# Differential attention by token tile, woven into its two projections, with three changes at the stage boundaries

## The chip, the cores and the metric

The kernel runs on one core of a Trainium2 chip. The metric is the device time of one execution in microseconds (us), the median of several runs. The five engines of the core are named as the profile names them: PE (TensorE, matmuls), DVE (VectorE), ACT (ScalarE), POOL (GpSimd) and SP (SyncE, which here only issues transfers).

## The reference

256 tokens of width 1024 pass through two transformer layers and a hybrid block. The change is in the second layer's differential attention and in how each stage hands over to the next. The attention computes, for 8 heads of two score maps each (64 wide) and values 128 wide:

```python
q = (x @ w_q).reshape(B, S, 2 * H, DH).transpose(0, 2, 1, 3) * (DH ** -0.5)
lam = jnp.exp(jnp.sum(lv[0] * lv[1])) - jnp.exp(jnp.sum(lv[2] * lv[3])) + lam_init
...
s = jnp.einsum('bhqd,bhkd->bhqk', qi, k_sh).astype(jnp.float32)
s = jnp.where(key_pos[None, :] <= qpos[:, None], s, -jnp.inf)
a = jax.nn.softmax(s, axis=-1).reshape(B, H, 2, Q_BLOCK, S)
diff = a[:, :, 0] - lam * a[:, :, 1]
return jnp.einsum('bhqk,bhkv->bhqv', diff.astype(v_sh.dtype), v_sh)
...
o = rms_norm(o, subln) * (1.0 - lam_init)
return o @ w_out
```

## The kernel before

The tokens form two tiles of 128 (tile 0 and tile 1). The network is a row of stages, in this order: F0, MI, MO, F1, P0, KV, F2, DQ, the attention, DO, F3, P1, HI, HC, HA, HO. F0 to F3 are feed-forward blocks, DQ and DO the query and the output projection of the differential attention, P0 and P1 gated projections, KV the shared keys and values, HI to HO the hybrid block. Each float32 matmul of a projection is done as three: a rounded high part and a remainder of both operands (`w_hi`, `w_lo`, `xT_hi`, `xT_lo`) are multiplied as hi by hi, lo by hi and hi by lo.

Weights come in slots of 512 KB (128 partitions by 2048). SP issues the transfers into `w_raw` (3 buffers), ACT casts a slot to `w_hi` (L536), POOL subtracts to get `w_lo` in four parts (L507), and there are 6 split slots. ACT's casts stand at fixed places of its program: `ahead(slot)` casts the slot four ahead. A projection of 1024 by 1024, DQ or DO, is 4 slots; each slot is 12 matmuls of 512 columns for one tile (`across_tile`, L1593 to L1595: four k, three matmuls each). Each engine's program is written out by hand, and each engine runs it strictly in order; semaphores tie them.

A stage boundary works so: ACT takes the sums of squares of a tile's output (`post_sum`), DVE makes the norm and adds into the residual (`boundary`, L1055 and L1056), PE transposes the residual (`t_of_x`, L1640), DVE scales the transposes by the gain, ACT rounds them to `xT_hi` (`t_hi`), DVE subtracts to get `xT_lo` (L1021). `pre_sum` and `pre_norm` make the following stage's norm. The transposes land in the PSUM banks that `t_bank` names. PSUM has eight banks: `acc` (4), `gu` (2), `tb` (2).

In the attention, one step handles one head for both tiles: PE computes four score blocks into `tb` (a = 0, partitions 0 to 63 of the operands) and `gu` (a = 1, partitions 64 to 127) (L1923), DVE adds the mask and takes the maxima, writing the scores to SBUF (L1308), ACT does four exps (L783), DVE forms the difference of the two softmaxes (L1315 to L1325), PE transposes it (L1931), ACT copies it (L791), PE multiplies by the values (L1940 to L1942), ACT copies the result (L797) and sums its squares (L802). The steps are pipelined over three to four heads; between DQ's last matmul and DO's first one nothing else stands on PE.

Of the kernel before, what the change touches and what calls it, by code (L numbers as in the profile page):

```python
# [26 lines left out]
I32 = mybir.dt.int32  # L27
# [15 lines left out]
AHEAD = 4  # L43
PART = 512
# [68 lines left out]

def psum_units(u):

    return u + 1 - (4 if u >= 4 * T["HC"] else 0)


def program(nc, A, out):
    ctx = ExitStack()  # L120
    with ctx:
# [60 lines left out]
        sc_ = area(6144, 2, 768)  # L182
        dif = area(7680, 2, LCOLS)
        difT = area(8448, 2, LCOLS)
# [50 lines left out]
        bg_bc = sb("bg_bc", [P, 8])  # L235

# [103 lines left out]
        d_lamexp = sem("d_lamexp")  # L340
        d_qn_ready = sem("d_qn_ready")
# [37 lines left out]
        def _(sp):  # L379
# [57 lines left out]
            def linear(s0, w, cols, halves_first=False):  # L437
# [3 lines left out]
                if halves_first:  # L441
                    order = [(c, j) for j in range(2) for c in cols]
# [22 lines left out]
            linear(S["DO"], A["diff_w_out"][0], both, halves_first=True)  # L465
# [35 lines left out]


# [20 lines left out]
        def _(act):  # L523
# [23 lines left out]
            def sum_of(j, t, src):  # L547
                if 2 * j + t:
                    act.wait_ge(sums_ready, 2 * j + t)
                nc.scalar.activation(squares[:], src, ACT.Square,  # L550
                                     accum_out=ssq[:, 2 * j + t:2 * j + t + 1]).then_inc(sums_ready, 1)
# [17 lines left out]
            def boundary(following, post_sum, between=lambda: None, late=lambda: None):  # L569
# [192 lines left out]
            def diff():  # L762
                s0 = S["DQ"]
                ahead(At(s0 + 1))
# [3 lines left out]
                for w in range(4):  # L768
                    if w == 2:
                        ahead(At(s0 + 3))  # L770
                    act.wait_ge(d_pl_in_psum, w + 1)
                    nc.scalar.copy(qT[:, 4 * (w % 2):4 * (w % 2) + 4, tok(w // 2)],
                                   tb[:, w % 2, :].rearrange("p (k c) -> p k c", k=4)).then_inc(d_pl_ready, 1)
                for step in range(DH + 3):
                    h = step
                    if h < DH:
                        act.wait_ge(d_negmax, 4 * h + 4)
                        for t in range(TILES):
                            for a in range(2):

                                e = sc_[:, h % 2, LCOLS * a + P * t:LCOLS * a + P * t + P * (t + 1)]
                                i = 2 * t + a
                                ins = nc.scalar.activation(e, e, ACT.Exp, scale=-1.0, bias=dstat[:, h % 2, 4 + i:5 + i],  # L783
                                                           accum_out=dstat[:, h % 2, 8 + i:9 + i])
                        ins.then_inc(d_exped, 1)
                    h = step - 2
                    if 0 <= h < DH:
                        act.wait_ge(d_dt_in_psum, h + 1)
                        if h >= 2:
                            act.wait_ge(d_o_in_psum, h - 1)  # L790
                        nc.scalar.copy(difT[:, h % 2, :], acc[:, 0, 512 * (h % 2):512 * (h % 2) + LCOLS]  # L791
                                       ).then_inc(d_dt_ready, 1)
                    h = step - 3
                    if 0 <= h < DH:
                        act.wait_ge(d_o_in_psum, h + 1)
                        src = acc[:, 1, 512 * (h % 2):512 * (h % 2) + 2 * P].rearrange("p (t c) -> p t c", t=2)
                        nc.scalar.copy(qn[:, :, tok(h)], src)  # L797
                        if h:
                            act.wait_ge(d_o_ready, h)
                        for t in range(TILES):  # L800
                            i = 8 * (h // 4) + 4 * t + h % 4
                            ins = nc.scalar.activation(squares[:, tok(t)], src[:, t, :], ACT.Square,  # L802
                                                       accum_out=hstat[:, i:i + 1])
                        ins.then_inc(d_o_ready, 1)
                act.wait_ge(d_o_ready, DH)
                t_hi("DO", 0)
                t_hi("DO", 1)
                out_linear("DO", "F3")
# [132 lines left out]
            for w in range(4):  # L941
# [4 lines left out]
                if w == 1:  # L946
# [5 lines left out]
            ahead(At(S["F2"]))  # L952
            ffn("F2", "DQ")
            act.wait_ge(x_ready, x_count(4, 1, 1))
            load_gain(A["norm_g"][1, 3])
            act.dma_start(lamv, A["diff_lambda"][0].rearrange("(o a) d -> o (a d)", o=1).broadcast_to([P, 256])
                          ).then_inc(d_landed, 16)
            act.dma_start(subln, A["diff_subln"].rearrange("o d -> d o")).then_inc(d_landed, 16)
# [11 lines left out]
        def _(dve):  # L970
# [24 lines left out]
            def norm_steps(j, t):  # L995
                i = 2 * j + t
                dve.wait_ge(sums_ready, i + 1)
# [1122 lines left out]
```

## Time and profile before

| | |
|---|---|
| median of 3 runs | 1438.81 us (1438.66 to 1441.03) |
| the profiled execution's own time | 1435.71 us |
| its span | 1433.8 us |
| PE busy | 1379.3 us (96%) |
| POOL busy | 1135.1 us (79%) |
| ACT busy | 659.8 us (46%) |
| DVE busy | 461.1 us (32%) |
| mean granted TensorE clock | 0.988 |

Busy times are sums over the whole span. The differential attention with its two projections is a small part of it, so its own stretches have to be read for what it costs. Brackets in a timeline row give the idle time of the engine ahead of that row and what ended it; a duration there is from the start of the record to its end, and where matmuls follow each other the distance of two starts is what one costs.

### The profile page before, as it was taken

The page shows a single profiled execution, that of the slowest core. Times are in us where ns is not written, and L with a number is a line of the kernel's source. Part 1 is how long each engine was busy: PE and PEld are TensorE (multiplying, and loading weights), DVE is VectorE, ACT ScalarE, POOL GpSimd, SP SyncE. Part 2 cuts the span into 40 slices and gives each one's busy share as a digit, 9 for nine tenths or more (in the row PEclk, how much of TensorE's full clock was granted, in tenths as well). Part 3 has the DMA queues.
Part 4 walks back from the last instruction along what each step waited for, and adds up shares of the span by engine and source line. Part 5 has one row for each costly group of instructions (what it writes and reads, how often), then busy time and mean ns, then how long its engine had stood idle before and what let it go on. Part 6 is the DMA issues. An engine that isn't in the chain of part 4 may idle for free.

```text
span 1433.8 us, 18162 instructions
## 1 busy us (share of the span) xinstructions
PE 1379.3 (96%) x6396; PEld 1128.4 (79%) x6396; DVE 461.1 (32%) x1108; ACT 659.8 (46%) x763; POOL 1135.1 (79%) x912
## 2 busy tenths in 40 slices
PE   7999999989999999999999889999999999999997
PEld 5888887877888878888887667888878777788785
DVE  6010044463011064200113665101056134552234
ACT  5444345445344455443344665434455443544431
POOL 5999978649999868899987418999877976679873
PEclk9999999999999999999999899999999999999999
DMA  8666545426656546565555406665554554347541
GB/s 260 206 210 208 197 149 189 147 90 207 202 183 197 181 157 193 182 204 177 190 191 176 136 1 191 205 192 189 180 180 154 184 168 147 119 146 235 184 142 42
DMA packets 160669, 246.95 MB, mean 172 GB/s; under 512 B 8892, under 2 KB 99812, under 8 KB 160484
## 3 DMA queue, kind: packets, MB, share of 16 engines
q1 hardware_dynamic: 158324, 239.42, 51.2%
q10 hardware_dynamic: 2288, 6.75, 1.3%
q8 instruction: 37, 0.61, 0.2%
q14 instruction: 20, 0.16, 0.0%
HBM read 245.10 MB, written 1.05 MB: 172 GB/s over the span
## 4 chain that ended last, share of the span: by engine, by line
POOL 59%; PE 19%; issue 19%; DMA 1%; ACT 1%; DVE 1%; POOLq 0%; SPq 0%; ACTq 0%; DVEq 0%
POOL w_lo L507 59%; PE acc L1593 5%; PE acc L1595 5%; PE acc L1594 5%; PE gu L1976 1%; DMA w_raw<-in_w_ffn_in 1%; ACT w_hi L536 1%; PE tb L1985 1%; PE tb L2011 0%; PE tb L1593 0%; PE tb L1595 0%; PE tb L1594 0%; PE gu L1595 0%; PE gu L1594 0%; PE gu L1593 0%
## 5 line engine op out<-in xcount | busy, mean ns | idle before, releaser
L507 POOL TENSOR_TENSOR w_lo<-w_raw,w_hi 128x512 fp32r<-128x512 f32 x896 | 1130.0, 1303 | 274.7 <-ACT w_hi L536 274.7
L536 ACT CAST w_hi<-w_raw 128x2048 fp32r<-128x2048 f32 x225 | 425.0, 1908 | 119.3 <-DMA w_raw<-in_w_ffn_in 33.0
L1593 PE MATMUL gu<-w_hi,xT_hi 128*128 128x512 f32 x832 | 331.3, 398 | 7.2 <-DVE xT_lo L1021 2.9
L1595 PE MATMUL gu<-w_hi,xT_lo 128*128 128x512 f32 x832 | 325.8, 392 | 0.0
L1594 PE MATMUL gu<-w_lo,xT_hi 128*128 128x512 f32 x832 | 325.5, 391 | 0.0
L1593 PE MATMUL acc<-w_hi,xT_hi 128*128 128x512 f32 x544 | 217.8, 400 | 3.9 <-DVE xT_lo L1021 2.6
L1595 PE MATMUL acc<-w_hi,xT_lo 128*128 128x512 f32 x544 | 212.6, 391 | 0.0
L1594 PE MATMUL acc<-w_lo,xT_hi 128*128 128x512 f32 x544 | 212.1, 390 | 0.0
L1593 PEld LDWEIGHTS gu<-w_hi,xT_hi 128*128 128x128 f32 x832 | 157.3, 189 | 39.9 <-POOL w_lo L507 3.4
L1595 PEld LDWEIGHTS gu<-w_hi,xT_lo 128*128 128x128 f32 x832 | 157.2, 189 | 33.5
L1594 PEld LDWEIGHTS gu<-w_lo,xT_hi 128*128 128x128 f32 x832 | 157.6, 189 | 31.4 <-issue 0.2
L1081 DVE SCALAR_TENSOR_TENSOR arena<-gu,rstd,arena 128x256 f32<-128x256 f32 x88 | 42.3, 484 | 370.6 <-ACT arena L610 370.3
L610 ACT ACTIVATE arena<-gu,rstd 128x256 f32<-128x256 f32 x88 | 41.3, 474 | 204.5 <-PE gu L1595 203.9
L1593 PEld LDWEIGHTS acc<-w_hi,xT_hi 128*128 128x128 f32 x544 | 102.5, 189 | 25.1 <-issue 4.4
L1595 PEld LDWEIGHTS acc<-w_hi,xT_lo 128*128 128x128 f32 x544 | 102.3, 188 | 22.0
L1594 PEld LDWEIGHTS acc<-w_lo,xT_hi 128*128 128x128 f32 x544 | 102.5, 188 | 19.8 <-issue 0.2
L1620 PE MATMUL acc<-w_hi,hT_hi 128*128 128x512 f32 x336 | 103.8, 390 | 0.0
L1626 PE MATMUL acc<-w_hi,hT_lo 128*128 128x512 f32 x336 | 103.7, 390 | 0.0
L1623 PE MATMUL acc<-w_lo,hT_hi 128*128 128x512 f32 x336 | 103.5, 389 | 0.0
L1088 DVE TENSOR_TENSOR hT_lo<-tb,hT_hi 128x512 fp32r<-128x512 f32 x40 | 27.7, 692 | 208.3 <-ACT hT_hi L626 208.3
L626 ACT CAST hT_hi<-tb 128x512 fp32r<-128x512 f32 x40 | 23.4, 585 | 123.2 <-PE tb L1675 123.2
L1626 PEld LDWEIGHTS acc<-w_hi,hT_lo 128*128 128x128 f32 x336 | 63.1, 188 | 13.1
(296 smaller groups left out, 1219.6 us busy)
## 6 DMA issues: line engine op xcount, KB each, us to landing
w_raw<-in_w_ffn_in SPq DMA_DIRECT2D x176, 512.0 KB, 4.6
w_raw<-in_w_ffn_out SPq DMA_DIRECT2D x88, 512.0 KB, 4.1
w_raw<-in_w_in SPq DMA_DIRECT2D x80, 512.0 KB, 4.4
w_raw<-in_mlstm_w_in SPq DMA_DIRECT2D x24, 512.0 KB, 4.3
w_raw<-in_w_ple_gate SPq DMA_DIRECT2D x16, 512.0 KB, 4.2
w_raw<-in_w_kv SPq DMA_DIRECT2D x16, 512.0 KB, 4.7
w_raw<-in_mlstm_w_out SPq DMA_DIRECT2D x8, 512.0 KB, 4.4
w_raw<-in_diff_w_q SPq DMA_DIRECT2D x8, 512.0 KB, 4.3
```

The lines of the kernel that those rows point to most:

```text
L507: ins = pool.tensor_tensor(w_lo[:, slot.spl, cols], w_raw[:, slot.raw, cols], w_hi[:, slot.spl, cols].bitcast(F32), ALU.subtract)
L536: nc.scalar.copy(w_hi[:, slot.spl, :], w_raw[:, slot.raw, :]).then_inc(hi_ready, 1)
L610: nc.scalar.activation(sg[:, t, :], gu[:, t, 0:CH], ACT.Silu, scale=rstd[:, 2 * m + t:2 * m + t + 1]).then_inc(silu_ready, 1)
L626: nc.scalar.copy(hT_hi[:], tb[:, 0, :].rearrange("p (k c) -> p k c", k=2)).then_inc(ht_hi_ready, 1)
L1081: v.scalar_tensor_tensor(hs[:, t, :], gu[:, t, CH:2 * CH], rstd[:, 2 * m + t:2 * m + t + 1], sg[:, t, :], ALU.mult, ALU.mult).then_inc(h_r ...
L1088: v.tensor_tensor(hT_lo[:], tb[:, 0, :].rearrange("p (k c) -> p k c", k=2), hT_hi[:].bitcast(F32), ALU.subtract).then_inc(ht_lo_ready, 1)
L1593: mm(out, xh, wh, start=(half == 0 and k == 0), stop=False)
L1594: mm(out, xh, wl, start=False, stop=False)
L1595: last = mm(out, xl, wh, start=False, stop=(half == 1 and k == 3))
L1620: mm(acc[:, t, 512 * half:512 * half + 512], a_hi[:, k, tok(t)], w(w_hi, half), start=st, stop=False)
L1623: mm(acc[:, t, 512 * half:512 * half + 512], a_hi[:, k, tok(t)], w(w_lo, half), start=False, stop=False)
L1626: last = mm(acc[:, t, 512 * half:512 * half + 512], a_lo[:, k, tok(t)], w(w_hi, half), start=False, stop=sp_)
```

## The change

It has two parts. The first rewrites `diff()` on all engines. The attention becomes 12 steps: steps 0 to 3 are tile 0 with two heads each (128 keys), steps 4 to 11 are tile 1 with one head each (256 keys). A step's scores stand in one PSUM bank, `gu[:, i % 2]`. The mask is put there first by a matmul of a bf16 identity with a bf16 mask, the scores of a = 0 and then those of a = 1 are accumulated on it; the latter wait for the former (`d_scores_low`). DVE takes all maxima of a step in one reduction from PSUM, ACT's exps read and write PSUM in place, DVE's difference reads PSUM. The values' products go to `acc` and stay there; squares and norm are taken per group of four heads. PE's program puts half slots of DQ for tile 1 (`q_part`) between the pieces of tile 0's steps, and half slots of DO for tile 0 (`o_part`) between those of tile 1's steps; a half slot is 6 matmuls of 512 columns. ACT, not DVE, scales the queries. DO's slots come column by column instead of half by half. POOL builds mask and identity in bf16 at the program's start.

The second part changes three things at stage boundaries. In the stages of `LOW_LAST`, a slot's eight matmuls with `xT_hi` come first and the four with `xT_lo` last, with the wait for `xT_lo` between them. `t_bank` gives `acc` for DO and for tile 1 of P0 and P1. And ACT and DVE make the following stage's norm of tile 0 (`pre_sum`, `pre_norm`) ahead of tile 1's `post_sum` and norm.

```diff
+LOW_LAST = ("F0", "F1", "F2", "F3", "MI", "MO", "DQ", "P0", "P1", "KV")
...
-            return acc[:, t, 512 * half:512 * half + 512] if q in ("KV", "HI", "HA", "HO") else tb[:, half, :]
+            if q in ("KV", "HI", "HA", "HO", "DO") or (q in ("P0", "P1") and t):
+                return acc[:, t, 512 * half:512 * half + 512]
+            return tb[:, half, :]
...
+            pool.wait_ge(consts_ready, 10)
+            pool.memset(mask_bf[:, 1, :], 0.0).then_inc(d_mask_ready, 1)
+            for i in range(4):
+                pool.tensor_copy(mask_bf[:, 0, tok(i)], causal[:, 0:P]).then_inc(d_mask_ready, 1)
...
                 t_hi(following, 0)
+                pre_sum(following, 0)
                 late()
                 post_sum(1)
-                pre_sum(following, 0)
...
+                def exps(i):
+                    t, hh = d_step(i)
+                    act.wait_ge(d_negmax, i + 1)
...
+                for i in range(4, D_STEPS):
+                    exps(i)
+                    if i >= 6:
+                        turned(i - 2)
+                    if i == 5:
+                        t_hi("DO", 0)
+                    if i == 6:
+                        ahead(At(S["DO"]))
...
-                pre_norm(following, 0)
-                pre_norm(following, 1)
+                    if not t or last_norm:
+                        pre_norm(following, t)
...
+                def maxima(i):
+                    t, hh = d_step(i)
+                    dve.wait_ge(d_scores, i + 1)
+                    n = len(hh)
+                    v.tensor_reduce(dstat[:, i % 2, 0:2 * n], gu[:, i % 2, :].rearrange("p (k c) -> p k c", k=2 * n),
+                                    AX, ALU.max, negate=True).then_inc(d_negmax, 1)
...
+                for i in range(D_STEPS):
+                    maxima(i)
+                    if i not in (0, 4):
+                        difference(i - 1)
+                    if i == 3:
+                        difference(i)
+                        link(sums(0))
+                    if i == 5:
+                        finish(0)
+                    if i == 10:
+                        link(sums(2))
+                difference(D_STEPS - 1)
+                finish(1)
...
+                if low_last:
+                    has_t(q, t, half)
+                    for k in range(4):
+                        wh, _, _, xl = operands(k)
+                        last = mm(out, xl, wh, start=False, stop=(half == 1 and k == 3))
...
+                def scores(i):
+                    t, hh = d_step(i)
+                    if i >= 2:
+                        pe.wait_ge(d_dif_ready, i - 1)
...
+                    mm(gu[:, i % 2, :], ident_bf[:], mask_bf[:, t, :], start=True, stop=False)
+                    for k, h in enumerate(hh):
+                        ins = mm(d_score(i, 0, k, w), qT[0:64, h, tok(t)], kT[0:64, h, 0:w], start=False, stop=False)
+                    ins.then_inc(d_scores_low, 1)
...
+                for i in range(6, D_STEPS):
+                    turn(i - 2)
+                    scores(i)
+                    if i == 6:
+                        t_of_o(0)
+                    else:
+                        n = i - 7
+                        o_part(n // 2, n % 2)
+                    scores_high(i)
+                    values(i - 2)
```

The helpers of the new PE program that the steps below name are these: `turn(i)` is two transposes of step i's difference into `tb`, `values(i)` its two products with the values, `scores_high(i)` the scores of a = 1, and `t_of_o(t)` the eight transposes of the attention's output of a tile. On DVE, `finish(t)` is the last sum of squares, the norm in eleven small operations, two multiplications over 512 columns and the four scalings of `t_of_o`'s transposes by tile t.

On PE, before, one head of the attention reads so: the next head's scores, then the transposes of an earlier one, then an earlier one's products with the values.

```order
L1923 MATMUL tb<-arena 128x128 [waits d_negmax]
L1923 MATMUL gu<-arena 128x128
L1923 MATMUL tb<-arena 128x256
L1923 MATMUL gu<-arena 128x256
L1931 MATMUL acc<-ident,arena 128x128 [waits d_dt_ready,d_dif_ready]
L1931 MATMUL acc<-ident,arena 128x128 x2
L1940 MATMUL acc<-arena 128x128 [waits d_o_ready,d_dt_ready]
L1941 MATMUL acc<-arena 128x128
L1942 MATMUL acc<-arena 128x128
```

After the change, step i = 7 of the same engine reads so: transposes of step 5, mask and low scores of step 7, a half slot of DO for tile 0, high scores of step 7, values of step 5.

```order
L2061 MATMUL tb<-ident,arena 128x128 [waits d_dt_ready,d_dif_ready]
L2061 MATMUL tb<-ident,arena 128x128
L2041 MATMUL gu<-mask_bf,ident_bf 128x512 [waits d_pl_ready,d_dif_ready]
L2043 MATMUL gu<-arena 128x256
L2012 MATMUL acc<-w_hi,xT_hi 128x512 [waits t_lo_ready,lo_ready]
L2013 MATMUL acc<-w_lo,xT_hi 128x512
L2014 MATMUL acc<-w_hi,xT_lo 128x512
L2012 MATMUL acc<-w_hi,xT_hi 128x512
L2013 MATMUL acc<-w_lo,xT_hi 128x512
L2014 MATMUL acc<-w_hi,xT_lo 128x512
L2052 MATMUL gu<-arena 128x256 [waits d_scores_low]
L2072 MATMUL acc<-arena 128x128 [waits d_dt_ready]
```

The two parts of the scores now stand apart with other work between them, and the values of step i - 2 stand right behind the high scores of step i.

On ACT, after the change, the same stretch of the program (steps 6 and 7) reads so; L825 are the exps, L833 the copy of the transposed difference, L573 the cast of a weight slot.

```order
L825 ACTIVATE gu,arena<-gu,arena 128x256 [waits d_negmax]
L825 ACTIVATE gu,arena<-gu,arena 128x256
L833 COPY arena<-tb 128x256 [waits d_o_in_psum,d_dt_in_psum]
L573 CAST w_hi<-w_raw 128x2048 [waits slot_used,raw_landed1]
L825 ACTIVATE gu,arena<-gu,arena 128x256 [waits d_negmax]
L825 ACTIVATE gu,arena<-gu,arena 128x256
L833 COPY arena<-tb 128x256 [waits d_o_in_psum,d_dt_in_psum]
```

The copy for step i - 2 stands behind the exps of step i, which wait for that step's maxima (`d_negmax`).

## Rows read from the trace of the kernel before

**Rows 1.** The windows view, core 0; busy us and count by engine, clock, DMA

```profile
core 0: us, PE busy (x) PEld busy (x) DVE busy (x) ACT busy (x) POOL busy (x), PEclk, DMA share, GB/s
800.00:840.00 40.00, 29.27 (x172) 21.19 (x170) 29.26 (x132) 30.37 (x119) 10.80 (x9) 0.83 0.25 79
840.00:880.00 40.00, 35.17 (x157) 28.43 (x158) 25.98 (x69) 20.63 (x25) 24.71 (x20) 0.94 0.34 106
```

**Rows 2.** PE's timeline: query projection, attention, output projection; start us, us

```profile
780.47 0.47 PE L1593 MATMUL acc<-w_hi,xT_hi 128*128 128x512 f32 x1 [0.41 <-POOL w_lo L507]
...
826.39 0.38 PE L1923 MATMUL tb<-arena 64*128 64x256 f32 x1
826.39 0.38 PE L1923 MATMUL gu<-arena 64*128 64x256 f32 x1
...
826.61 0.38 PE L1923 MATMUL tb<-arena 64*128 64x256 f32 x1
...
827.73 0.55 PE L1931 MATMUL acc<-ident,arena 128*128 128x128 f32 x3 [0.74 <-DVE arena L1325]
...
828.81 0.39 PE L1942 MATMUL acc<-arena 128*128 128x128 f32 x2
...
841.98 0.47 PE L1593 MATMUL acc<-w_hi,xT_hi 128*128 128x512 f32 x1 [2.62 <-DVE xT_lo L1021]
```

**Rows 3.** PE's timeline, one woven step of the hybrid block

```profile
1185.12 0.39 PE L1595 MATMUL acc<-w_hi,xT_lo 128*128 128x512 f32 x1
1185.44 0.92 PE L1976 MATMUL gu<-arena 64*128 64x128 f32 x4
1186.29 0.55 PE L1985 MATMUL tb<-ident,arena 128*128 128x128 f32 x3
1186.67 0.33 PE L1997 MATMUL gu<-arena 128*128 128x64 f32 x2
...
1187.26 0.48 PE L1593 MATMUL acc<-w_hi,xT_hi 128*128 128x512 f32 x1
```

**Rows 4.** ACT's timeline, one head of the differential attention and the next

```profile
829.05 0.40 ACT L783 ACTIVATE arena<-arena 128x128 f32<-128x128 f32 x1
...
829.83 0.49 ACT L783 ACTIVATE arena<-arena 128x256 f32<-128x256 f32 x1
...
830.33 0.49 ACT L783 ACTIVATE arena<-arena 128x256 f32<-128x256 f32 x1
...
831.17 0.36 ACT L797 COPY arena<-acc 128x256 f32<-128x256 f32 x1
...
832.11 0.40 ACT L783 ACTIVATE arena<-arena 128x128 f32<-128x128 f32 x1
```

**Rows 5.** The page's costliest groups: count, busy us, mean ns, idle before

```profile
L507 POOL TENSOR_TENSOR w_lo<-w_raw,w_hi 128x512 fp32r<-128x512 f32 x896 | 1130.0, 1303 | 274.7 <-ACT w_hi L536 274.7
L536 ACT CAST w_hi<-w_raw 128x2048 fp32r<-128x2048 f32 x225 | 425.0, 1908 | 119.3 <-DMA w_raw<-in_w_ffn_in 33.0
```

**Rows 6.** Groups of ACT and DVE by form, the whole span

```profile
L550 ACT ACTIVATE squares<-acc 128x1024 bf16<-128x1024 f32 x16 | 16.4, 1023 | 8.6 <-DVE acc L1119 5.6 <-PE acc L1626 3.0
...
L1175 DVE TENSOR_REDUCE arena<-arena 128x4 f32<-128x512 f32 x2 | 1.4, 688 | 0.1
...
L1325 DVE SCALAR_TENSOR_TENSOR arena<-arena 128x256 f32<-128x256 f32 x8 | 3.8, 478 | 0.0
...
L991 DVE TENSOR_TENSOR arena<-arena 128x8 f32<-128x8 f32 x6 | 1.0, 167 | 0.2
```

**Rows 7.** PE's timeline at P0's tile 1 and in F3

```profile
522.28 0.50 PE L1593 MATMUL tb<-w_hi,xT_hi 128*128 128x512 f32 x1 [2.30 <-DVE xT_lo L1021]
...
529.47 0.62 PE L1620 MATMUL acc<-w_hi,pT_hi 128*128 128x512 f32 x2
...
876.13 0.77 PE L1593 MATMUL gu<-w_hi,xT_hi 128*128 128x512 f32 x1 [1.47 <-DVE xT_lo L1021]
...
884.12 0.39 PE L1595 MATMUL gu<-w_hi,xT_lo 128*128 128x512 f32 x1
```

More of the change, by code:

```diff
@@ L765, in diff @@
+                evacuate(0, 0)
+                evacuate(0, 1)
                 act.wait_ge(d_lam, 1)
                 nc.scalar.activation(lamp[:, 2:4], lamp[:, 0:2], ACT.Exp).then_inc(d_lamexp, 1)
-                ahead(At(s0 + 2))
[L768 to L804, printed above, removed]
@@ L1582, in across_tile, with operands @@
                     pe.wait_ge(lo_ready, slot.count())
-                if q:
+                low_last = q in LOW_LAST and not by_part
+                if low_last:
+                    has_t_hi(q, t, half)
+                elif q:
                     has_t(q, t, half)
+                def operands(k):
+                    return (w_hi[:, slot.spl, 512 * k:512 * k + 512], w_lo[:, slot.spl, 512 * k:512 * k + 512],
+                            xT_hi[:, 4 * half + k, tok(t)], xT_lo[:, 4 * half + k, tok(t)])
                 for k in range(4):
@@ new lines, in diff, with half_slot @@
+                s0 = S["DQ"]
+                def half_slot(slot, half, part, t, out):
+                    pe.wait_ge(lo_ready, slot.count())
+                    if part == 0 and slot.s in (S["DQ"], S["DQ"] + 1):
+                        has_t("DQ", t, half)
+                    elif part == 0 and slot.s in (S["DO"], S["DO"] + 1):
+                        has_t("DO", t, half)
+                    for k in (2 * part, 2 * part + 1):
+                        wh = w_hi[:, slot.spl, 512 * k:512 * k + 512]
+                        wl = w_lo[:, slot.spl, 512 * k:512 * k + 512]
+                        xh, xl = xT_hi[:, 4 * half + k, tok(t)], xT_lo[:, 4 * half + k, tok(t)]
+                        mm(out, xh, wh, start=(half == 0 and k == 0), stop=False)
+                        mm(out, xh, wl, start=False, stop=False)
+                        last = mm(out, xl, wh, start=False, stop=(half == 1 and k == 3))
+                    if part == 1:
+                        last.then_inc((tile0_used, slot_used)[t], 1)
@@ new lines, in q_part, with o_part, turn_q @@
+                def q_part(i, part):
+                    half_slot(At(s0 + i), i % 2, part, 1, acc_outs(i // 2, 1))
+                def o_part(i, part):
+                    half_slot(At(S["DO"] + i), i % 2, part, 0, acc_outs(i // 2, 0))
+                def turn_q(t, half):
+                    pe.wait_ge(d_qn_ready, 2 * t + half + 1)
+                    for k in range(4):
+                        ins = nc.tensor.transpose(acc[:, t, 512 * half + P * k:512 * half + P * k + P],
+                                                  qn[:, t, tok(4 * half + k)], ident[:])
+                    ins.then_inc(d_pl_in_psum, 1)
@@ new lines, in diff @@
+                for i in range(4):
+                    across_tile(At(s0 + i), i % 2, 0, acc_outs(i // 2, 0), "DQ" if i < 2 else None)
+                    if i == 2:
+                        t_of_x("DQ", 1)
+                q_part(0, 0)
+                turn_q(0, 0)
+                turn_q(0, 1)
+                q_part(0, 1)
+                pe.wait_ge(d_mask_ready, 8)
+                pe.wait_ge(d_lam, 1)
+                scores(0)
+                q_part(1, 0)
+                scores_high(0)
@@ new lines, in diff @@
+                scores(1)
+                q_part(1, 1)
+                scores_high(1)
+                q_part(2, 0)
+                q_part(2, 1)
+                turn(0)
+                scores(2)
+                q_part(3, 0)
+                scores_high(2)
+                turn(1)
+                values(0)
+                scores(3)
+                q_part(3, 1)
+                scores_high(3)
+                values(1)
+                turn_q(1, 0)
+                turn(2)
+                turn_q(1, 1)
@@ L1961, in hybrid @@
+                turn(D_STEPS - 2)
+                o_part(2, 1)
+                values(D_STEPS - 2)
+                turn(D_STEPS - 1)
+                o_part(3, 0)
+                values(D_STEPS - 1)
+                o_part(3, 1)
+                t_of_o(1)
+                for i in range(4):
+                    across_tile(At(S["DO"] + i), i % 2, 1, acc_outs(i // 2, 1), "DO" if i < 2 else None)
+                    if i == 2:
+                        t_of_x("F3", 0)
             def hybrid():
```

337 lines of the change are left out of this document (197 added, 140 removed).

## Prediction

> **What bounds the kernel now.** I read the page first: PE is busy 96% of the span, and between the stages' ends its matmuls of 512 columns follow each other every 0.2275 us. Two things can therefore move the time: PE's own work, and the places where PE stands. The windows view shows where it stands most: from 800 to 840 us, which is the attention, PE is busy 29.27 of 40 us and POOL, which makes the weights' remainders, only 10.80, at a mean clock of 0.83; from 840 to 880 it is 35.17 of 40 at 0.94 [rows 1]. So the attention is the one stretch where POOL has nothing to do (all six slots are full) and where PE waits for ACT and DVE. PE's timeline shows how: per head it waits 0.74 us for DVE's difference, and DO's first matmul comes after 2.62 us of idle behind `xT_lo` [rows 2]. ACT's timeline shows the beat, 3.06 us from one head's first exp to the next one's (829.05 to 832.11), without idle between [rows 4]: ACT sets the pace there, with four exps in 1.77 us and the copies and squares in the rest.
>
> I measure the change over one stretch: from the last matmul before DQ, 780.1 us (0.41 us of idle before 780.47 [rows 2]), to the end of the first 48 matmuls of F3, 884.12 + 0.23 = 884.35 [rows 7]. That is 104.25 us before.
>
> **PE's work in that stretch after the change.** DQ and DO for two tiles and F3's first two slots are 240 matmuls at 0.2275: 54.6 us. 56 transposes (8 of the residual, 16 of queries, 16 of outputs, 16 for F3) at 0.12, a little under the 0.38 us for three in the hybrid's step (1186.29 to 1186.67 [rows 3]): 6.7. Each of the 12 steps has a mask matmul of 512 columns, 0.23, which no row shows in bf16 and which I price as any matmul of 512 columns; the scores, before run as pairs: the records on `tb` and `gu` both start at 826.39, and the next pair at 826.61, so 256 columns of both maps cost 0.22 a pass and two passes 0.43 [rows 2]. After the change the high map waits for the low one, so the two no longer share that time and cost 0.86; two transposes of the difference 0.21; two products with the values 0.43 (0.22 each, from 828.81 to the end of that pair [rows 2]). That is 1.73 a step, 20.8 in all.
>
> The weaving adds changes between products over 64 partitions and over 128. The hybrid's step prices them: into the 64-row products the matmul before takes 0.32 instead of 0.23 (1185.12 to 1185.44), the four passes of 0.107 take 0.85, which leaves 0.42 for the change between halves and the way out, 0.2 each, and the first matmul after a step lasts 0.48 instead of 0.39 [rows 3]. Low and high each pay 0.29, 0.58 a step and 7.0 in 12, and 16 half slots pay 0.09 on coming back, 1.4: together 8.4. A rule speaks to this: the Trainium skill, TensorEngine Tiling (Array Packing), Key Properties, says that changing the tiling mode drains TensorE while different tiles run in parallel. Both halves of the rule stand in the rows (0.2 on leaving, the shared start at 826.39); were the drains free, the sum would be 7 us lower.
>
> PE's work is so 54.6 + 6.7 + 20.8 + 8.4 = 90.5 us.
>
> **Where PE would stand.** The order of the programs decides, and each wait is a chain of rows. In tile 1's steps 7 to 11, `values(i-2)` stands on PE right behind `scores_high(i)` and waits for the copy of step i-2, which stands on ACT behind `exps(i)`, which wait for the maxima of the very scores just issued. The chain: the scores leave PE, 0.25; one reduction over 512 columns, 0.70 (688 ns [rows 6]); two exps of 256, 0.98 (829.83, 830.33 [rows 4]); the copy of 256 columns, 0.37 [rows 4]; two handovers of 0.05. That is 2.40 us a step, 12.0 for five, and behind it stand the next step's transposes and half slot, which can't fill it. DVE's difference of step i-1, a small operation of 167 ns and two passes over 256 columns of at most 478 ns each [rows 6], runs meanwhile and is hidden. In step 6 the maxima stand on DVE behind `finish(0)`, with its eleven operations linked at 0.20 (167 ns each [rows 6]) and 512-wide passes: 3.88. On tile 0 `turn(1)`, right behind `scores_high(2)`, waits for max and difference, which is here a small operation and four passes over 128 columns, together 1.40 (two passes over 256 are 0.96 [rows 6], and four start-ups cost more than two): 0.25 + 0.70 + 1.40 = 2.35; `turn(2)` the same with some work between, 1.23; `scores(4)` 0.50; `turn(4)` behind a cast of 1.91 us [rows 5] that delays the exps of step 4, 3.23. Transposes of tile 0's output in step 6 wait for `finish(0)`: 2.55. At the end nothing covers the chain of step 11, squares 0.6 (half of the 1023 ns for 1024 columns and a start-up [rows 6]), sum 0.7, eleven operations 2.25, product 0.7 and then transposes, scaling, cast and subtraction, of which the end is paid at DO's first and second half: of this chain of some 7 us about 2 lie beside `o_part(3, 1)` and the last products, and 5.05 remain. DQ's boundary 1.02 and F3's 3.03 (before 1.47 before F3's first matmul [rows 7] and two smaller gaps) are near to before. Sum: 12.0 + 3.88 + 2.35 + 1.23 + 0.50 + 3.23 + 2.55 + 5.05 + 1.02 + 3.03 = 34.8.
>
> Work and waits are 125.3 us, 21.0 more than before. What the change removes (ACT's copies of the output, 0.36 [rows 4], DVE's writing of the scores, the ends of two projections) lies on ACT and DVE, which are no longer the pace: PE's own order is. The exps in PSUM, which no row shows, I price as in SBUF; their bounds are 0.1 us less and 0.1 more each, 1.3 us over the stretch. The Trainium skill, VectorE: DVE Perf Modes, in its section on the errata, gives ScalarE 172 cycles plus columns from PSUM against 224 from SBUF; by that 32 exps would be 1.4 us shorter, an estimate that no row here shows.
>
> **The clock.** Idle stretches cost more than themselves. After the 2.30 us gap at 522.28 the next 24 matmuls took 7.19 us (to 529.47) instead of 5.46, that is 1.7 more [rows 7]. The stretch before already holds such falls (0.83 and 0.94 [rows 1]). A step of 7 to 11 is 1.73 + 0.58 + 6 × 0.2275 + 0.09 of work and 2.40 of waiting, 6.2 us; with such a gap in each, I take about three more falls, 5 us, between 0 and 10.
>
> **The boundary changes.** Elsewhere `low_last` can cover at most DVE's last subtraction at a gap, and the `acc` bank lets P0's and P1's transposes of tile 1 land earlier: of the 2.30 us [rows 7] I take half, 1.2, at both, and 1.7 of clock at P0. Against it ACT now squares 1024 columns, 1.2 us with the reading of its sum (1023 ns [rows 6]), ahead of `late()` and tile 1's `post_sum`, at every boundary: where tile 1's chain ends last, at KV and HI, it costs those 1.2 each, at MI 0.6; F1 gains 0.3. Sum: -1.2 - 1.7 - 1.2 + 1.2 + 1.2 + 0.6 - 0.3 = -1.4; bounds: minus 6 (all these gaps closed) and plus 6. Moving the loads of `lamv` and `subln` before F2 costs nothing: they are small, nothing is queued behind them but F2, and their wait is past; POOL's bf16 mask is made in the first microseconds.
>
> **Sum.** 1435.71 + 21.0 + 5 - 1.4 = 1460.3 for an execution like the profiled one. The median of the runs stands 3.10 above that execution, so 1463.4, rounded 1463.
>
> **Rivals.** *Faster:* the copy's wait on PE could be short after all, because PE is already late when it comes to `values(i-2)`. It decides at a point that can be named: PE's waits in the stretch must come below 104.25 - 90.5 = 13.8 us. The five waits of 2.40 alone are 12.0, and the ends of both projections cannot be covered. If the waits of steps 6 to 11 all vanished (-15.9) and the clock stayed up, the time would be 1463 - 15.9 - 5 - 7 (free drains) = 1435. For it speaks that POOL's idle stretch and the ends of DQ and DO are covered by the weave; against it the order of the rows. Chance 0.06. *No change:* the same waits vanish and the clock stays up, but the drains cost what the rows say: 1442, 0.03. *Milder, still slower:* drains free (-7) and no new clock falls (-5), the same waits: 1451, between 1443 and 1455; chance 0.22, since both prices come from one other stage. *Worse:* the clock stays at half through the woven steps, as it did for 24 matmuls at P0. Steps 6 to 11 hold 6 × 3.77 = 22.6 us of work, which would take twice as long, 17 us more than the 5 allowed: 1480, between 1475 and 1485; chance 0.12. *Weights late:* a slot needs 1.91 us of ACT and 4 × 1.30 of POOL [rows 5], and F3's casts stand between the steps of the attention; POOL's 5.2 us a slot is less than what PE takes for one in this stretch (12 matmuls a tile and a step's chains between), so it would show only behind the last casts, for up to 5 us, and lies inside the range.
>
> **How the numbers follow.** Forecast 1463, its own range 1455 to 1473 (waits -4 to +3 by the bounds of drains, exps and reductions, clock 0 to 10, boundaries), chance 0.57. With most of the milder case and half of the worse one the range is 1447 to 1480; it leaves out the faster and the unchanged case, 0.09, and the ends of both others, about 0.1. A measurement of this kernel can tell 0.2% from no change, about 3 us. Faster 0.06, same 0.03, slower 0.91.
>
> **What would show it.** In PE's timeline: L2072 with idle of about 2.4 us ended by ACT in each of steps 7 to 11 (right), or under 0.5 (the step on the order fails). Scores of L2043 and L2052 not overlapping, and 0.2 lost after each (drains). The stretch to the 48th matmul of F3 near 130 us with clock. The windows view of the attention at a clock under 0.85. Wrong would be the prediction if ACT's exps ended before PE came to the values, if the half clock lasted longer than the gaps, or if a boundary outside moved by more than 3 us.

## The result, and the profile after

The changed kernel takes 1477.77 us (median, 1473.38 to 1479.35) against 1439.92 for the kernel before, a ratio of 1.0252 with a 95% interval of 1.0237 to 1.0268. The forecast was 1463 in a range of 1447 to 1480: the sign and the place are right, the size is 15 us short.

The page after, its head, PE's row and the rows of 40 slices:

```profile
span 1475.0 us, 18122 instructions
PE 1409.5 (96%) x6408; PEld 1142.1 (77%) x6408; DVE 460.4 (31%) x1051; ACT 656.1 (44%) x735; POOL 1136.2 (77%) x920
...
PE   7999999899999999999999778999999999999997
...
PEclk9999999999999999999999668999999999999999
```

PE is busy 30 us more than before with 6408 instead of 6396 instructions, and three slices that stood at 8, 9 and 9 in the row of the granted clock now stand at 6, 6 and 8. Those slices are the attention. The windows view of the changed kernel from 840 to 880 us (columns as in [rows 1]):

```profile
840.00:880.00 40.00, 30.50 (x79) 17.82 (x80) 8.63 (x19) 8.57 (x27) 4.95 (x4) 0.59 0.08 27
```

The clock is 0.59 on average there: most of the time it is the lower of its two levels, 1.2 instead of 2.4 GHz. DVE and ACT are busy about a fifth of the time and POOL an eighth. PE's timeline over one step, from the values of step 5 to those of step 6:

```profile
850.21 0.49 PE L2072 MATMUL acc<-arena 128*128 128x128 f32 x2 [2.10 <-ACT arena L833]
850.53 0.39 PE L2074 MATMUL acc<-arena 128*128 128x128 f32 x2
850.75 0.38 PE L2061 MATMUL tb<-ident,arena 128*128 128x128 f32 x2
850.97 0.44 PE L2041 MATMUL gu<-mask_bf,ident_bf 128*128 128x512 bf16 x1
851.34 1.22 PE L2043 MATMUL gu<-arena 64*128 64x256 f32 x2
852.49 0.79 PE L2012 MATMUL acc<-w_hi,xT_hi 128*128 128x512 f32 x1
853.08 0.63 PE L2013 MATMUL acc<-w_lo,xT_hi 128*128 128x512 f32 x1
853.50 0.63 PE L2014 MATMUL acc<-w_hi,xT_lo 128*128 128x512 f32 x1
853.93 0.63 PE L2012 MATMUL acc<-w_hi,xT_hi 128*128 128x512 f32 x1
...
855.34 1.22 PE L2052 MATMUL gu<-arena 64*128 64x256 f32 x2
858.66 0.79 PE L2072 MATMUL acc<-arena 128*128 128x128 f32 x2 [2.10 <-ACT arena L833]
```

The bracket of the last row is the wait that was forecast, at its place: 2.10 us for ACT's copy, behind the high scores. The rows of the half slot, 853.08, 853.50 and 853.93, then show what was not forecast in its size: matmuls that follow each other by 0.43 us (0.2275 at the full clock). ACT and DVE in the same step, which are the links of the chain:

```profile
856.60 0.69 DVE L1363 TENSOR_REDUCE arena<-gu 128x2 f32<-128x512 f32 x1 [6.59 <-PE gu L2052]
```

```profile
857.33 0.45 ACT L825 ACTIVATE gu<-gu,arena 128x256 f32<-128x256 f32 x1 [7.17 <-DVE arena L1363]
...
858.24 0.37 ACT L833 COPY arena<-tb 128x256 f32<-128x256 f32 x1
```

Maxima 0.69, exps 0.91 with their accumulators, copy 0.37: the chain of the forecast, 0.3 shorter. Two rows of the view that sums PE's waits (us in total, times, longest):

```profile
PE acc L2072 <- ACT arena L833: 13.5, 6, 3.0
PE tb L2061 <- DVE arena L1382: 6.3, 3, 2.9
```

Over the stretch that the prediction measured, from DQ's first matmul (781.65 us, with no idle ahead of it) to the end of the 48th matmul of F3 (927.36), the time is 145.7 us; it was 104.25. All waits in it add up to 28.95 us.

### The profile page after: what moved, and what is told of

It reads as the page before. It is cut to its first block, busy times and chain, and to the rows that moved or that the text cites. A ratio compares the mean times of both kernels' runs of the same rounds, so it can differ in the third digit from the quotient of the medians.

```text
span 1475.0 us, 18122 instructions
## 1 busy us (share of the span) xinstructions
PE 1409.5 (96%) x6408; PEld 1142.1 (77%) x6408; DVE 460.4 (31%) x1051; ACT 656.1 (44%) x735; POOL 1136.2 (77%) x920
## 4 chain that ended last, share of the span: by engine, by line
PE 53%; POOL 30%; issue 9%; DVE 4%; ACT 2%; DMA 1%; POOLq 0%; ACTq 0%; SPq 0%; DVEq 0%
POOL w_lo L544 30%; PE gu L1684 6%; PE gu L1685 6%; PE gu L1687 6%; PE acc L1684 5%; PE acc L1687 5%; PE acc L1685 5%; PE acc L1717 3%; PE acc L1723 3%; PE acc L1720 3%; PE gu L2158 1%; PE acc L2012 1%; ACT w_hi L573 1%; PE acc L2013 1%; PE acc L2014 1%
## 5 line engine op out<-in xcount | busy, mean ns | idle before, releaser
L573 ACT CAST w_hi<-w_raw 128x2048 fp32r<-128x2048 f32 x225 | 424.9, 1907 | 118.6 <-DMA w_raw<-in_w_ffn_in 33.6
L1687 PE MATMUL gu<-w_hi,xT_lo 128*128 128x512 f32 x708 | 277.3, 392 | 0.0
L1684 PE MATMUL acc<-w_hi,xT_hi 128*128 128x512 f32 x512 | 206.5, 403 | 2.4 <-DVE xT_lo L1093 1.5
L1685 PE MATMUL acc<-w_lo,xT_hi 128*128 128x512 f32 x512 | 200.6, 392 | 0.0
L1687 PE MATMUL acc<-w_hi,xT_lo 128*128 128x512 f32 x488 | 191.7, 393 | 0.0
L1687 PEld LDWEIGHTS gu<-w_hi,xT_lo 128*128 128x128 f32 x708 | 133.5, 189 | 28.2
L1684 PEld LDWEIGHTS acc<-w_hi,xT_hi 128*128 128x128 f32 x512 | 97.2, 190 | 22.6 <-POOL w_lo L544 1.9
L1685 PEld LDWEIGHTS acc<-w_lo,xT_hi 128*128 128x128 f32 x512 | 97.3, 190 | 18.8 <-issue 0.2
L1687 PEld LDWEIGHTS acc<-w_hi,xT_lo 128*128 128x128 f32 x488 | 92.2, 189 | 20.0
L1720 PEld LDWEIGHTS acc<-w_lo,hT_hi 128*128 128x128 f32 x336 | 63.1, 188 | 13.1
```

What stands on the lines that cost most here:

```text
L573: nc.scalar.copy(w_hi[:, slot.spl, :], w_raw[:, slot.raw, :]).then_inc(hi_ready, 1)
L1684: mm(out, xh, wh, start=(half == 0 and k == 0), stop=False)
L1685: mm(out, xh, wl, start=False, stop=False)
L1687: last = mm(out, xl, wh, start=False, stop=(half == 1 and k == 3))
L1720: mm(acc[:, t, 512 * half:512 * half + 512], a_hi[:, k, tok(t)], w(w_lo, half), start=False, stop=False)
```

## The experiments

Every ratio is to the kernel before, run beside it on the same chip. Two bounds in brackets behind a ratio are its 95% interval. The changed kernel stands at 1.0252.

**e3, the waits filled.** Does the idle bring the low clock, or does the woven work? Transposes whose results nobody reads are put into the wait, and nothing else is changed.

```diff
                     scores_high(i)
+                    for _ in range(18):
+                        nc.tensor.transpose(tb[:, 1, 128:256], ident[:], ident[:])
                     values(i - 2)
```

> The changed kernel, with 18 transposes of the identity into an unused part of tb put on PE between the high scores of step i and the values of step i-2, for i = 6 to 11 (their results are not used). At full clock they take 1.93 us, which lies inside the wait of 2.1. Theory A (the idle brings the half clock): the step's chain is unchanged, PE is busy meanwhile, the clock in the woven steps rises to 0.9 or more, and a step takes 6.3 us instead of 8.75: five or six steps give 12 to 15 us back, 1463. Theory B (the half clock belongs to the woven work): the fillers run at half clock too, 3.9 us each time instead of 2.1, and the time rises by 6 * 1.8 = 11 us: 1488.

Measured: 1462.63 us, ratio 1.0163 (1.0146 to 1.0180). Work was added and the kernel became 13 to 15 us faster. Its windows view and PE's timeline:

```profile
840.00:880.00 40.00, 36.64 (x212) 26.94 (x212) 14.51 (x38) 11.40 (x31) 7.51 (x7) 1.00 0.09 27
```

```profile
855.74 2.19 PE L2130 MATMUL tb<-ident 128*128 128x128 f32 x18
857.91 0.49 PE L2072 MATMUL acc<-arena 128*128 128x128 f32 x2
```

The clock is 1.00 over the same 40 us, the fillers take 2.17 us where 2.10 were idle, and `values` runs when it ran before, relative to its scores: the chain is as long as ever. A step takes 6.1 us (857.91 to 863.99) instead of 8.7 (four steps from 850.21 to 884.96 in the changed kernel). Theory B, that the woven work itself holds the clock down whatever it waits for, is refuted for these steps; 2.6 us a step were the clock's.

**e1 and e2, the order on ACT and DVE.** e2 turns ACT's order round, e1 ACT's and DVE's.

```diff
                 for i in range(4, D_STEPS):
-                    exps(i)
                     if i >= 6:
                         turned(i - 2)
+                    exps(i)
...
                 for i in range(D_STEPS):
+                    if i >= 6:
+                        difference(i - 1)
                     maxima(i)
-                    if i not in (0, 4):
+                    if i not in (0, 4) and i < 6:
                         difference(i - 1)
```

> The changed kernel, with only ACT's order turned round (the copy of step i-2 before the exps of step i). Theory A: the copy is early, but on DVE the difference of step i-1 still stands behind the maxima of step i, so the transposes of step i-1 now wait for it: 0.25 + 0.70 + 1.2 - 0.43 of values in between, about 1.8 us a step instead of 2.1. The clock stays near 0.6 and the time falls by 1 to 4 us: 1475. Rival (the place of ACT's copy alone is the cause): 1452 to 1464.

> The changed kernel, with two orders turned round in tile 1's steps: ACT copies the transposed difference of step i-2 before the exps of step i, and DVE forms the difference of step i-1 before the maxima of step i. Theory A (PE's waits behind the high scores are the cause, and they bring the half clock with them): the waits of about 2.1 us in steps 7 to 11 fall below 0.5, six of them worth about 13 us, and the granted clock from 840 to 885 us rises from 0.6 to over 0.9, worth about another 12: 1477 - 25 = 1452, between 1445 and 1458. Theory B (the half clock belongs to the woven work itself, whatever it waits for): only the waits go, 1464, and the clock stays near 0.6. Theory C (another wait takes the place of the one removed): 1470 to 1478.

Measured: e2 1471.55, ratio 1.0210 (1.0190 to 1.0230); e1 1462.29, ratio 1.0167 (1.0145 to 1.0189). In e2 the wait for the copy is gone and another stands in its place, as expected, though shorter, 0.8 to 1.3 us a step against 1.8; the kernel became 6 us faster, where 1 to 4 were expected:

```profile
855.87 0.44 PE L2061 MATMUL tb<-ident,arena 128*128 128x128 f32 x2 [1.32 <-DVE arena L1382]
...
862.87 0.44 PE L2061 MATMUL tb<-ident,arena 128*128 128x128 f32 x2 [1.31 <-DVE arena L1382]
```

In e1 both are gone. But its windows view reads

```profile
840.00:880.00 40.00, 36.30 (x112) 22.49 (x113) 14.62 (x38) 11.80 (x32) 6.93 (x6) 0.67 0.08 26
```

and from 840 to 850 us PE was busy 10.00 of 10.00 us at a granted clock of 0.50. Theory A was half right: the waits of steps 7 to 11 are worth about what they last, but taking them away didn't bring the clock back, and e1 missed its 1452 by 10 us. The number is that of theory B (1464), yet theory B can't hold beside e3. What is left to try is where the clock fell: ahead of these steps.

**e5 and e6, no fall on the way in.** e5 is e1 with fillers of the same kind in the earlier waits (20 ahead of `turn(1)`, 10 ahead of `turn(2)`, 25 ahead of `turn(4)`, 11 ahead of `t_of_o(0)`). e6 also fills the waits around `t_of_o(1)`, with 27 and 14, and moves one cast and one group's squares on ACT behind the exps of steps 5 and 4. The edit on ACT:

```diff
-                ahead(At(s0 + 3))
-                squares_of(1)
                 for i in range(4, D_STEPS):
...
+                    if i == 4:
+                        squares_of(1)
                     if i == 5:
+                        ahead(At(s0 + 3))
                         t_hi("DO", 0)
```

> The kernel of e1 (both orders turned round), with transposes of the identity put into PE's waits ahead of tile 1's steady steps: 20 ahead of the transposes of step 1, 10 ahead of those of step 2, 25 ahead of those of step 4 and 11 ahead of tile 0's output transposes (results unused). Nothing is added in steps 7 to 11, where e1 has hardly any wait. In e1 the clock fell in those early waits and stayed at half from 830 to 866 us with PE busy 100%. Theory A1 (the early waits bring the fall, and the woven steps without waits only fail to lift it): the clock stays over 0.95 from 810 to 880 us; e1 has some 44 us at half clock there, 37 of them busy, so 18 us come back: 1444, between 1440 and 1449. Theory B (the woven steps bring the clock down by themselves): it falls again after 835 us, and the time is 1453 to 1462.

> The kernel of e5, with two more edits: transposes of the identity in the waits around tile 1's output transposes (27 and 14), and ACT's cast of the last slot of DO moved from ahead of the exps of step 4 to behind those of step 5. By A1 the clock also stays up at DO's tile 1 (0.67 from 880 to 890 us in e1, worth 3) and the wait ahead of step 4's transposes shrinks by up to 1.9: 1440, between 1435 and 1445. If e5 stays near 1460, this stays within 5 us of it.

Measured: e5 1452.6 in the median, ratio 1.0086 (1.0050 to 1.0122), but its executions fall in two groups, 1448.16 and 1448.47 against 1458.38 and 1459.45; e6 1445.64, ratio 1.0067 (1.0032 to 1.0101), with seven of its nine executions from 1442.44 to 1450.17 and two at 1458.92 and 1463.04. Theory A1 had 1444 for e5 and 1440 for e6: both medians lie above its bounds. In e6 the time goes with the mean granted clock of the execution, from 1442.44 us at 0.996 to 1463.04 at 0.981. The profiled execution of e5 is one of the long ones. Its PE timeline shows waits close together in step 6 (0.94 us ahead of `t_of_o(0)`, then the two brackets of 1.18 and 0.91 below), and behind them the scores at half clock (1.22 us for what took 0.70 at 828.16). The 0.36 in the last row is no wait: the record of the mask's matmul, whose weight load stands at 836.01, is missing there.

```profile
834.20 0.49 PE L2074 MATMUL acc<-arena 128*128 128x128 f32 x2 [1.18 <-ACT arena L833]
...
835.83 0.60 PE L2063 MATMUL tb<-ident,arena 128*128 128x128 f32 x2 [0.91 <-DVE arena L1382]
836.78 1.22 PE L2045 MATMUL gu<-arena 64*128 64x256 f32 x2 [0.36 <-issue]
```

From there matmuls ran at half clock until 863 us. In e6's profile the clock fell at the same place but rose at about 840 us, and the woven steps then ran at full clock without any filler among them:

```profile
840.00:880.00 40.00, 39.31 (x204) 29.46 (x205) 22.97 (x54) 14.82 (x36) 13.35 (x11) 0.99 0.17 53
```

```profile
840.81 0.49 PE L2075 MATMUL acc<-arena 128*128 128x128 f32 x2
...
844.73 0.49 PE L2075 MATMUL acc<-arena 128*128 128x128 f32 x2
```

So woven steps without waits run at either level. All three profiles enter them at the lower one; in e1 it lasted from 838.5 to 866 us and in e5 from 836.8 to 863, while in e6 it rose again after some 5 us. A step of e6 is 3.92 us, all work. What decides how soon the clock rises is not settled by these runs. ACT's edit made e6's waits ahead of this place shorter (0.24 instead of 0.94 us ahead of `t_of_o(0)`, 0.60 instead of 0.91 ahead of the transposes), but e6 too has two long executions, so these waits alone are not shown to decide it.

**e10 and e11, the order on PE.** The mildest cure: the half slot is put behind the high scores instead of ahead of them, for steps 7 to 11, and so into the wait.

```diff
-                        o_part(n // 2, n % 2)
-                    scores_high(i)
+                        scores_high(i)
+                        o_part(n // 2, n % 2)
+                    if i == 6:
+                        scores_high(i)
                     values(i - 2)
```

> The changed kernel with one order turned round on PE: in steps 7 to 11 the high scores come directly behind the low ones and the half slot behind both, so that the half slot (1.4 us at full clock, 2.6 at half) lies inside the wait of 2.1 us for the values. Theory A (the wait behind the high scores, and the clock with it): if the clock stays at half, as in e1, the wait is gone and only the time of waiting comes back, 5 * 2.1 = 10, 1467; if the clock rises, 1455. Rival (the high scores now wait for the low ones to leave PE, about 0.25 a step, and the wait for the values is as long as before because its chain starts with the later of the two): 1475 and more.

> The kernel of e6 with the order of e10 on PE. There is no long wait left in e6, and its clock is at full in these steps. The high scores directly behind the low ones save one way into and out of the 64-partition products a step, 0.29 * 5 = 1.5 us by the prediction's price, and cost up to 0.25 * 5 = 1.3 for the wait between them: within 2 us of e6, 1445.

Measured: e10 1455.73, ratio 1.0111 (1.0092 to 1.0130); e11 1446.08, ratio 1.0030 (1.0018 to 1.0042). In e10, PE's timeline:

```profile
853.75 0.49 PE L2072 MATMUL acc<-arena 128*128 128x128 f32 x2 [0.51 <-ACT arena L833]
...
854.83 0.70 PE L2043 MATMUL gu<-arena 64*128 64x256 f32 x2
855.58 0.70 PE L2052 MATMUL gu<-arena 64*128 64x256 f32 x2
856.21 0.50 PE L2012 MATMUL acc<-w_hi,xT_hi 128*128 128x512 f32 x1
...
858.38 0.49 PE L2072 MATMUL acc<-arena 128*128 128x128 f32 x2 [0.50 <-ACT arena L833]
```

The wait is 0.50 us, the high scores start 0.75 us behind the start of the low ones, of which 0.43 are the two passes, and a step takes 4.63 us; from 850 to 870 us the granted clock is 1.00. Here too the steps were entered at the lower level, and it rose at about 845 us. One order, nothing else, gives back 20 of the 38 us. In e11, on e6, where nothing was left to cover, it changes nothing beyond the noise, as expected (1446.08 against 1445.64).

**e4, e7, e8 and e9, the boundary changes on the kernel before.** e4 has all three, e7 `low_last` alone, e8 the order of sums and norms alone, e9 `low_last` and the bank. The edits are those of the diff above, applied to the kernel before, without the bank for DO; e9 leaves out these lines and what belongs to them on DVE:

```diff
                 t_hi(following, 0)
+                pre_sum(following, 0)
                 late()
                 post_sum(1)
-                pre_sum(following, 0)
```

> The kernel before, with the boundary changes alone (low_last, acc for tile 1 of P0 and P1, the following stage's norm of tile 0 earlier; the attention and DO as before). The prediction's terms give -1.4 us against the kernel before, so 1438.5; the landmarks of the changed trace outside the attention (P0 -2.9, P1 -1.3, HI -0.5, MI +0.7, F1 +1.1, KV +1.0) give -1.9, so 1438. Rival (the boundary changes cost, and carry part of the 38 us): over 1443.

> The kernel before with low_last alone. e4 is 6.2 us faster than before, and its landmarks put -2.9 at P0, -3.3 at F3 and -1.3 at P1. If low_last is the cause (the four matmuls with the low part last, so that 8 matmuls or 1.8 us of work lie ahead of the wait for xT_lo, and the clock does not fall at P0 and F3): 1433 to 1435. If it needs the acc bank for tile 1, P0 and P1 keep their 2.30 us: 1436 to 1437.

> The kernel before with the order alone: ACT's sum and DVE's norm of the following stage's tile 0 ahead of tile 1's. The prediction gave it a cost of up to 1.2 us a boundary, +2.7 in all; so 1441 to 1443. Rival (it lies beside PE's work and changes nothing): 1440.

> The kernel before with low_last and with acc for tile 1 of P0 and P1, but the old order of sums and norms. e7 (low_last alone) is 4.0 us faster than before and keeps 2.30 us of wait at P0 and P1; e4 (all three) has no such wait there, and e8 shows that the order costs 4.5. If the three are independent: 1440.9 - 4.0 - 2 * 2.5 = 1432, a ratio of 0.9935, and faster than e4 (0.996). Rival (the bank works only with the order, whose earlier norm gives DVE the time): no better than e7, 0.997.

Measured: e4 1433.68, ratio 0.9960 (0.9946 to 0.9974); e7 1436.35, 0.9972 (0.9959 to 0.9986); e8 1443.79, 1.0031 (1.0016 to 1.0047); e9 1429.48, 0.9929 (0.9915 to 0.9942). Expected were 1438, 1433 to 1437, 1441 to 1443 and 1432. The bank: at P0 tile 1's transposes now go to `acc` ahead of tile 1's own work, and the wait of 2.30 us and the half clock behind it [rows 7] are gone. PE's timeline of e9 there:

```profile
519.86 1.03 PE L1659 MATMUL acc<-ident,x_res 128*128 128x128 f32 x8
520.65 0.48 PE L1606 MATMUL tb<-w_hi,xT_hi 128*128 128x512 f32 x1
```

The order: the residual that tile 1's transposes need is late by a norm, so a wait of 0.74 stands ahead of them, and without the bank the one for `xT_lo` is there as well. PE's timeline of e8 at P1:

```profile
1071.72 0.66 PE L1667 MATMUL tb<-ident,x_res 128*128 128x128 f32 x4 [0.74 <-DVE x_res L1068]
1074.51 0.80 PE L1614 MATMUL tb<-w_hi,xT_hi 128*128 128x512 f32 x1 [2.13 <-DVE xT_lo L1033]
```

and with it the first matmul lasts 0.80 instead of 0.50: this boundary, which kept its clock in the profile before (behind a wait of 2.30 us, as at P0, where it fell), loses it. `low_last`: at F3 the wait of 1.47 us before the first matmul [rows 7] becomes 0.65 and the clock stays up in the profiles of e4 and e7; in that of e9 it fell there all the same (0.83 from 870 to 880 us). PE's timeline and the window from 870 to 880 us (before: 0.75) of e4:

```profile
875.64 0.47 PE L1614 MATMUL gu<-w_hi,xT_hi 128*128 128x512 f32 x1 [0.65 <-ACT xT_hi L577]
875.95 0.39 PE L1615 MATMUL gu<-w_lo,xT_hi 128*128 128x512 f32 x1
```

```profile
870.00:880.00 10.00, 7.89 (x37) 5.98 (x36) 8.59 (x23) 6.29 (x9) 10.00 (x9) 1.00 0.66 199
```

**e12, the weave with e9's boundaries.** e6 with the order of sums and norms put back.

> The kernel of e6 (woven attention, all long waits removed or filled) with the old order of sums and norms at the boundaries, so that its boundaries are those of e9. If the order costs here what it costs in e8 (4.5 us), the time is 1441, equal to the kernel before, and the difference to e9 (1429.5), about 11 us, is the price of the weave at a full clock: the mask matmuls, the scores no longer run in pairs, and the ways in and out of the 64-partition products, 2.8 + 4 + 8 by the prediction's prices. If it comes to 1435 or less, that price is smaller and the weave would pay with its waits gone.

Measured: 1445.72, ratio 1.0049 (1.0026 to 1.0072), with executions from 1439.08 to 1457.28. The expected 4.5 us are not there, and its interval overlaps that of e6; the spread is wider than the effect. Against e9 the woven attention costs 16 us in the median. Even the fastest execution of e12 (1439.08, the profiled one), whose clock was 0.995, lies 9.6 above e9's median, and at the same mean clock of 0.991 e12 took 1445.15 and 1445.72 us, e9 1429.07 to 1429.48.

## Why the prediction was right in sign and 15 us short

- *PE's order makes the waits*: right. L2072 waited for ACT in each of steps 7 to 11, 2.10 four times and 2.17 once, against 2.40. In all the waits were 28.95 us against 34.8. Of the chain's 0.3 us, 0.07 are the exps' (0.91 against 0.98) and 0.2 the scores' way out, priced at 0.25, while DVE started 0.04 us behind their end; the tail of tile 0's norm in step 6 was over-priced by another 2.2. e2, e1 and e10 show by orders alone that the chain was named rightly.
- *PE's work, 90.5 us*: right within 4. What is left of the measured stretch without its waits and its clock is 145.7 - 28.95 - 22.3 = 94.5 us. The price of a step of 7 to 11 was 1.73 + 0.58 + 1.37 + 0.09 = 3.77, and e6 shows 3.92 without waits. The prices of the 64-partition products hold at full clock: in e10 the high scores take 0.63 us to the next matmul (855.58 to 856.21), 0.43 of passes and 0.20 for the way out, and that matmul lasts 0.50 instead of 0.39. The drain that the rule of the Trainium skill (TensorEngine Tiling (Array Packing), Key Properties) names for a change of mode fits the 0.20 on the way out. It doesn't cover the 0.32 between low and high scores, which are two tiles of one mode and between which PE also waits for a semaphore (`d_scores_low`).
- *The clock, +5 between 0 and 10*: this is the step that failed: the term was sized at 5 and measured 22. Summed over the windows of 10 us from 810 to 910 us, PE's busy time times one minus the granted clock is 22.3 us in the changed kernel. I had priced each fall by the one at P0, 1.7 us, after which work without waits follows, and had counted three. Here a wait of 2.1 us came every 8.7 us, and the clock was below full in every window from 830 to 910. The sum had a flaw of its own too: the kernel before loses 7.5 us to the clock in the same stretch by the same reckoning (810 to 890 us), and its 104.25 us hold them, while I built the changed stretch at full clock and added 5. I so forecast a smaller loss than before's, under waits twice as long. The rival *Worse* had the right mechanism, at 1475 to 1485 with a chance of 0.12, and deserved more than the milder one. In the stretch the forecast was 104.25 + 21.0 + 5 = 130.25 us and 145.7 were measured: 17.3 more for the clock, 3.9 more for PE's work, 5.9 less for the waits. That the total was only 15 us short owes something to luck, since the over-priced waits hid a third of the clock's miss.
- *The boundary changes, -1.4 between -6 and +6*: the sign was right, the terms were not. e4 measured -5.8. What was missing is F3, where `low_last` saves 0.8 of wait and a fall of the clock, about 3 us; I had put F3's wait into the stretch as unchanged. The order's cost, +2.7 in the terms that I gave to ACT's square, was 4.5 in e8 (2.3 to 6.8 by its interval), of which 2.2 at P1 alone by its trace.
- *Exps in PSUM*: 0.1 less to 0.1 more each. The groups of the changed kernel by form read

```profile
L825 ACT ACTIVATE gu<-gu,arena 128x256 f32<-128x256 f32 x16 | 7.1, 447 | 35.6 <-DVE arena L1363 35.6
...
L825 ACT ACTIVATE gu<-gu,arena 128x128 f32<-128x128 f32 x16 | 5.4, 339 | 5.3 <-DVE arena L1363 5.3
```

against 0.49 and 0.40 us [rows 4]: 0.04 to 0.06 less each, 1.6 us over 32. The estimate by the cycles that the Trainium skill gives (VectorE: DVE Perf Modes, the section on the errata), 0.043 us each, agrees within 0.02; the page has them for results that go to SBUF, here they go to PSUM. For the total it mattered little: only what lies in the chain, 0.07 us a step, shortened PE's waits.

In the stretch of the prediction the 41.5 us (145.7 against 104.25) divide so: waits 28.95 against 15.8 (the sum of PE's idle times over 0.3 us in each), 13.2; clock 22.3 against 7.5, 14.8; and the rest, PE's work at full clock, 13.5. By the prediction's prices that rest would be 12 × 0.23 = 2.8 of mask matmuls; 5.1 for scores no longer in pairs (12 × 0.86, against 0.65 in each of eight heads, where 128 columns of both maps cost 0.11 a pass and 256 cost 0.22); and the 8.4 for the ways in and out of the 64-partition products less some 2.3 that the kernel before pays for its own eight, 6.1. That is 14. With the boundary changes worth -6 on the kernel before, the attention's rewriting costs some 44 us by difference. It was not run alone. With its long waits removed or filled, and at the same mean clock, the weave is still 16 us slower than the form before with the same boundaries (e12 against e9). Its fillers and waits, about 13 + 5 us, are no more than 2 us over e9's waits in the same stretch (16.6). That PE's work grew is so the likeliest reason, but it was reckoned, not isolated by a run.

## What to carry to other kernels

Where two engines run ahead of a third, look at what stands directly behind the instruction that starts a chain: the end of that chain must not be asked for before other work has been issued, and turning one order round on PE was worth 20 us here. Price a wait on PE together with the clock: here a wait that came back in every step cost its own 2.1 us and 2.6 us more, on 3.9 us of work. e3 shows the test: fill the wait with matmuls nobody needs. Measure a bundle's parts alone: the best kernel here, e9 at 0.9929, is two of the four parts on the kernel before.

## What was not expected of the hardware

- Matmuls nobody needs made the kernel 13 to 15 us faster: with 18 transposes in each wait of 2.1 us the granted clock from 840 to 880 us went from 0.59 to 1.00.
- The clock, once low, stayed low through work without waits: in e1 from 838.5 to 866 us, PE busy 10.00 of 10.00 us from 840 to 850 at 0.50. The same steps in e6 ran at 0.99 from 840 to 880 us. PE's busy time alone doesn't tell the clock, and executions of one kernel differ by it (e5: 1448 us at a mean of 0.992, 1459 at 0.984).
- The same wait can bring the lower level or not. Behind the first wait of 2.28 us in the attention, which e1 and e10 share with the same program up to there, e1's clock from 810 to 820 us was 0.66 and e10's 1.00.
